# mLSTM branch output as four block pairs of seven half-size products, merged tiles kept on the chip

## The chip, the cores and the metric

The kernel runs on one core of a Trainium2 chip. The metric is the device time of one launch in microseconds.

## What is computed

A decoder layer for 1024 tokens and a width of 1024, one sequence. Cut to what bears on the change:

```python
mod = silu(c) @ w_ada + b_ada                      # shift, scale, gate
h = rms_norm(x, g_norm) * (1 + scale) + shift
xa, va, oa, za, ia, fa, qa, ka, vat, zb, ga, gb = split(h @ w_in)
xc = silu(causal_depthwise_conv(xa, w_conv, b_conv))
h_m = mlstm_chunkwise(q, k, v from xc and va; gates ia, fa)      # 4 heads of 256
h_m = rms_norm(sigmoid(oa) * h_m, g_mlstm_head) + skip_mlstm * xc
y_m = (h_m * silu(za)) @ w_out_mlstm               # 1024 x 1024 @ 1024 x 1024
o_a = softmax-weighted sum of three dilated window attentions   # 4 heads of 128
y_a = (o_a * silu(zb)) @ w_out_attn                # 1024 x 512 @ 512 x 1024
merged = sigmoid(ga) * y_m + sigmoid(gb) * y_a
out = rms_norm(x + gate * (merged @ w_out), g_final)
```

## The kernel before

Every large product is made in three passes (`three_pass`, L590): each factor is held as a high part, rounded to the matmul's type, and a low part, what is left, and TensorE adds high x high, high x low and low x high. ScalarE writes high parts (a copy), GpSimd (POOL) or VectorE (DVE) low parts (a subtraction of two tiles in SBUF).

The program is a sequence of stages, each with hand-written instruction lists for SyncE (loads), GpSimd, TensorE, ScalarE and VectorE; semaphores tie them. Setup makes h; the blocks stage makes 28 pairs of output tiles of 128 channels, each pair by seven products of half the size in the order 5, 1, 2, 4, 6, 7, 3 (12 matmuls each, with sums of the weights ahead of them and sums of the products behind: 84 matmuls where the plain way takes 96); the mixing stage runs the four mLSTM heads and the attention; then follow **merge** (L1890) and **finish** (L2131). The change touches the end of mixing and these two.

End of mixing. `turn_stats` (L1177) on SyncE's queue stores a head's two tiles of the mLSTM branch to DRAM (L1182) and loads the softmax statistics `ct` (L1184). From them VectorE and ScalarE (`weigh_groups`, `group_exp`, L1545) make the weights of the three attention groups, which go through DRAM and come back as `qm` and `vt` (L1193); VectorE scales and adds with them (L1787 to L1807).

Merge. TensorE first makes the gates' plain products for output tiles 0 and 1 (`first_pairs`, 192 matmuls), then for each of the eight tiles m the mLSTM product `um` (2 token halves x 8 contraction tiles x 3 passes = 48 matmuls of 128x512) and the attention product `ua` (24). SyncE loads the eight tiles `um_lo_raw` (L1936) once all of the mixing is done, then four `ua` tiles, weights (L1919) and gates (L1925). ScalarE makes the high parts of the tiles (`split_high`, L2039), weights (`branch_high`, L2033) and output weights (`out_high`, L2043); VectorE the low parts (L2085, L2089); GpSimd the weights' (L1965). VectorE's `merge_tile` (L2104 to L2108) multiplies both products by their gates and adds them in `num`; ScalarE's queue stores the merged tile to DRAM (L2074).

Finish. GpSimd's queue loads merged columns of 128 tokens back (L2187, L2203) and GpSimd splits them (L2178 high, L2181 low). TensorE multiplies by the output weights, 8 token tiles of 2 x 24 matmuls. Behind the first 24 stands the gate sum (L2214), which waits for three rows that SyncE loads (gate, bg, gf, L2160 to L2162) at

```python
        sp.wait_ge(proj, BRANCH_DONE)
```

where BRANCH_DONE is the last mLSTM product of tile 7; the last attention product comes after it. ScalarE's queue loads rows of x (L2241) two counts later.

Of the kernel before, what the change touches and what calls it, by code (L numbers as in the profile page):

```python
# [9 lines left out]
P = 128  # L10
# [22 lines left out]
PAIRS0 = MERGE0 + 2 * PLAIN + 2 * KT  # L33
# [10 lines left out]
TOTAL = PRODUCTS * PAIRS  # L44
BY_POOL = 2
# [1027 lines left out]
def mix(nc, a, sem, ps, T):  # L1073
# [71 lines left out]
    def sync(sp):  # L1145
# [32 lines left out]
        def turn_stats(i):  # L1178

            for q in range(2):  # L1180
# [260 lines left out]
    def scalar(act):  # L1441
# [183 lines left out]
        group_exp(HEADS - 1)  # L1625

    def vector(dve):
# [760 lines left out]
```

## Time and profile before

| | us |
|---|---|
| median of 3 runs | 1370.97 (1370.72 to 1371.75) |
| the profiled execution | 1371.11 |
| its span, first to last instruction | 1369.3 |
| TensorE busy in the span | 1345.7 (98%) |
| VectorE busy | 855.3 (62%) |
| ScalarE busy | 580.1 (42%) |
| GpSimd busy | 463.0 (34%) |
| mean granted TensorE clock | 0.999 |

The span lies 1.8 us under the execution's time. A busy time counts records, and records of matmuls overlap, so that a full TensorE may be short of its peak. The stages stand in the trace at these times: mixing ends with transposes at 1097.8, the merge stage runs from there to 1273.4, the finish from there to the end.

### The profile page before, as it was taken

How to read it: one execution, taken by the hardware profiler on the slowest of the kernel's cores; microseconds unless marked ns; L12 is line 12 of the kernel's file. 1: busy time of each engine (PE TensorE's matmuls, PEld its weight loads, DVE VectorE, ACT ScalarE, POOL GpSimd, SP SyncE). 2: the span in 40 equal slices, each digit the busy share in tenths (PEclk: the TensorE clock that was granted, in tenths of full speed). 3: DMA queues.
4: the chain of work that ended last, by engine and by line, in shares of the span. 5: the costliest groups of instructions: out<-in, count | busy, mean ns of one | idle time of the engine just before them, and what ended most of it. 6: DMA issues, size and time to landing. Idle time of an engine off the chain costs nothing.

```text
span 1369.3 us, 17469 instructions
## 1 busy us (share of the span) xinstructions
PE 1345.7 (98%) x6453; PEld 1126.9 (82%) x6453; DVE 855.3 (62%) x1472; ACT 580.1 (42%) x1016; POOL 463.0 (34%) x298
## 2 busy tenths in 40 slices
PE   8999999999999999999999999999999999999998
PEld 6888888888888888888898788889878887888886
DVE  7988766573745444535368757866875766434586
ACT  7663353343444344332545446354545534111122
POOL 0096555554545555543002200210120022222551
PEclk9999999999999999999999999999999999999999
DMA  8522323323234343337231841553172165453543
GB/s 316 196 82 95 132 99 123 123 93 115 101 123 139 123 143 134 139 112 228 73 83 48 231 93 32 161 148 94 48 227 67 33 241 205 128 187 140 173 138 108
DMA packets 65454, 180.52 MB, mean 132 GB/s; under 512 B 22001, under 2 KB 22129, under 8 KB 63318
## 3 DMA queue, kind: packets, MB, share of 16 engines
q1 hardware_dynamic: 61082, 166.64, 36.9%
q10 hardware_dynamic: 3168, 8.70, 1.9%
q0 software_dynamic: 1120, 4.06, 1.0%
q8 instruction: 52, 0.85, 0.3%
q14 instruction: 32, 0.26, 0.1%
HBM read 132.49 MB, written 46.89 MB: 131 GB/s over the span
## 4 chain that ended last, share of the span: by engine, by line
PE 87%; DVE 6%; ACT 3%; DMA 2%; issue 1%; SPq 0%; POOL 0%; ACTq 0%; DVEq 0%
PE banks L592 23%; PE banks L594 23%; PE banks L593 23%; PE banks L1265 4%; PE banks L1390 2%; PE banks L1400 2%; PE banks L1350 2%; PE banks L1356 2%; DMA wraw<-in_w_all 1%; PE banks L1339 1%; PE banks L1348 1%; PE banks L1409 1%; PE banks L584 1%; PE banks L556 1%; PE banks L1378 1%
## 5 line engine op out<-in xcount | busy, mean ns | idle before, releaser
L1248 POOL TENSOR_TENSOR wlo<-wraw,whi 128x1024 fp32r<-128x1024 f32 x28 | 72.1, 2575 | 436.5 <-ACT whi L1468 411.1
L718 POOL TENSOR_TENSOR wlo<-w_sum,whi 128x512 fp32r<-128x512 f32 x112 | 165.2, 1477 | 137.4 <-ACT whi L843 137.4
L592 PE MATMUL banks<-t_hi,whi 128*128 128x512 f32 x448 | 174.3, 389 | 0.0
L593 PE MATMUL banks<-t_lo,whi 128*128 128x512 f32 x448 | 174.3, 389 | 0.0
L594 PE MATMUL banks<-t_hi,wlo 128*128 128x512 f32 x448 | 174.3, 389 | 0.0
L989 DVE TENSOR_TENSOR c_sum<-c_sum,banks 128x512 f32<-128x512 f32 x196 | 134.4, 686 | 44.7 <-PE banks L594 30.6
L592 PE MATMUL banks<-h_hi,whi 128*128 128x512 f32 x416 | 162.0, 389 | 0.0
L594 PE MATMUL banks<-h_hi,wlo 128*128 128x512 f32 x416 | 161.9, 389 | 0.0
L593 PE MATMUL banks<-h_lo,whi 128*128 128x512 f32 x416 | 161.8, 389 | 0.0
L843 ACT ACTIVATE whi<-w_sum 128x512 fp32r<-128x512 f32 x112 | 70.5, 630 | 165.5 <-PE banks L594 100.7
L592 PE MATMUL banks<-whi,h_hi 128*128 128x512 f32 x256 | 100.2, 391 | 1.4 <-POOL wlo L1248 1.4
L594 PE MATMUL banks<-whi,h_lo 128*128 128x512 f32 x256 | 99.7, 389 | 0.0
L593 PE MATMUL banks<-wlo,h_hi 128*128 128x512 f32 x256 | 99.6, 389 | 0.0
L593 PEld LDWEIGHTS banks<-t_lo,whi 128*128 128x128 f32 x448 | 84.1, 188 | 17.5
L594 PEld LDWEIGHTS banks<-t_hi,wlo 128*128 128x128 f32 x448 | 84.1, 188 | 17.4
L592 PEld LDWEIGHTS banks<-t_hi,whi 128*128 128x128 f32 x448 | 84.1, 188 | 17.4
L592 PEld LDWEIGHTS banks<-h_hi,whi 128*128 128x128 f32 x416 | 78.1, 188 | 16.3 <-POOL wlo L1248 0.2
L594 PEld LDWEIGHTS banks<-h_hi,wlo 128*128 128x128 f32 x416 | 78.1, 188 | 16.3
L593 PEld LDWEIGHTS banks<-h_lo,whi 128*128 128x128 f32 x416 | 78.1, 188 | 16.2
L865 ACT ACTIVATE fin<-c_sum 128x1024 f32<-128x1024 f32 x56 | 79.4, 1467 | 2.4 <-DMA chunk_decay_rows<-wlast 2.3
L718 POOL TENSOR_TENSOR wlo<-wraw,whi 128x512 fp32r<-128x512 f32 x42 | 63.0, 1507 | 48.8 <-ACT whi L843 48.8
L718 POOL TENSOR_TENSOR wlo<-raw,whi 128x512 fp32r<-128x512 f32 x42 | 58.5, 1402 | 51.3 <-ACT whi L843 51.3
(374 smaller groups left out, 2904.8 us busy)
## 6 DMA issues: line engine op xcount, KB each, us to landing
wraw<-in_w_all SPq DMA_DIRECT2D x72, 512.0 KB, 4.3
raw<-in_w_all SPq DMA_DIRECT2D x28, 512.0 KB, 4.4
queries_keys<-fin SPq DMA_DIRECT2D x12, 1024.0 KB, 4.0
qa<-queries_keys SPq DMA_DIRECT2D x12, 768.0 KB, 13.7
s_wada<-in_w_ada_cols SPq DMA_DIRECT2D x16, 512.0 KB, 8.2
attn_values<-fin SPq DMA_DIRECT2D x6, 1024.0 KB, 4.0
tn<-attn_values SPq DMA_DIRECT2D x12, 512.0 KB, 10.1
sig_c<-merge_gates SPq DMA_DIRECT2D x6, 1024.0 KB, 6.4
```

The costliest lines, as they stand in the source:

```text
L592: t_.matmul(out, w_hi, x_hi, start=first, stop=False)
L593: t_.matmul(out, w_hi, x_lo, start=False, stop=False)
L594: return t_.matmul(out, w_lo, x_hi, start=False, stop=last)
L718: nc.gpsimd.tensor_tensor(wlo4[:, o % 4, :], source(r, j), whi4[:, o % 4, :].bitcast(F32), subtract).then_inc(s_split, 1)
L843: A(whi4[:, o % 4, :], source(r, j), ACT.Copy).then_inc(s_high, 1)
L865: A(fin[r % 2][:, j, :].rearrange("p (r u) -> p r u", r=d), c_sum[:, r % 2, j, :].rearrange("p (u r) -> p r u", r=d), ACT.Sigmoid if r < Q ...
L989: v.tensor_tensor(out, x, bank(r, j), ALU.add).then_inc(part_added, 1)
L1248: nc.gpsimd.tensor_tensor(to, wraw[:, q % 2, :], hi.bitcast(F32), ALU.subtract).then_inc(w_split, 1)
L1265: mm = t_.matmul(ps[:, h, :], w[:, to, k * P:(k + 1) * P], x[:, k, h * HALF:(h + 1) * HALF], start=(e == 0), stop=(e == 3 * KT - 1))
L1350: mm = t_.matmul(M2[:, 0:DH + 1], qm[:, d, c * P:(c + 1) * P], cst[:, d, :], start=(d == 0), stop=(d == 1))
L1356: mm = t_.matmul((M1, M2)[d][:, 0:DH + 1], kw[:, c % 2, d * P:(d + 1) * P], v1[:, c, 0:DH + 1], start=True, stop=True)
L1390: mm = t_.matmul(A0[:, u * 2 * P:u * 2 * P + b * P], qa[:, g % 2, 0, t * P:(t + 1) * P], qa[:, g % 2, 1, (t + 1 - b) * P:(t + 1) * P], sta ...
```

## The change

The mLSTM branch's output product is made like the blocks: four pairs of output tiles, seven half-size products each. Token-side factors are the quarters of the branch (4 contraction tiles x 512 tokens) and sums of them: VectorE makes four differences (L2231 of the changed kernel) and seven low parts (L2236), each of 128x2048, ScalarE seven high parts (L2137, L2142). For each pair VectorE makes four weight sums (L2239) and seven joins into the on-chip tile `umo` (L2254), then multiplies by the gate. The attention products follow for all eight tiles, and `merge_tile` adds them into `umo` in place. GpSimd splits token columns straight out of `umo`; the merged tensor in DRAM is gone. Mixing ends with tiles 0 to 5 of the branch loaded by ScalarE's queue (L1651) and 6 and 7 copied on the chip by SyncE's. The gates come in halves; the output weights' tiles are made in the order 4 to 7, 0 to 3. BRANCH_DONE is now the last attention product.

```diff
-PAIRS0 = MERGE0 + 2 * PLAIN + 2 * KT
+PAIRS0 = MERGE0 + 2 * PLAIN + KT
...
+BRANCH_PAIRS = range(PAIRS, PAIRS + KT // 2)
+OUT_ORDER = (4, 5, 6, 7, 0, 1, 2, 3)
...
         def turn_stats(i):
-            for q in range(2):
+            for q in range(2) if i < HEADS - 1 else ():
                 sp.wait_ge(um_done, i * 2 + q + 1)
                 sp.dma_start(um_d[i, q], xc[:, q, :]).then_inc(um_out[q], 16)
             sp.wait_ge(stat_out, (i + 1) * 16 * sum(STATS))
             sp.dma_start(ct[:].rearrange("p g c w -> p g (c w)"), stat_d.rearrange("g (p c) w -> p g (c w)", c=NCH)).then_inc(ct_in, 16)
+            for q in range(2) if i == HEADS - 1 else ():
+                sp.wait_ge(um_done, 2 * HEADS - 1 + q)
+                sp.dma_start(T["um_raw"][:, KT - 2 + q, :], xc[:, q, :]).then_inc(T["tile_in"][KT - 2 + q], 16)
...
-        group_exp(HEADS - 1)
+        act.wait_ge(out_turned, 4 * HEADS)
+        for q in range(2):
+            act.wait_ge(um_out[q], 16 * HEADS)
+        for k in range(KT - 2):
+            act.dma_start(T["um_raw"][:, k, :], um_d[k // 2, k % 2]).then_inc(T["tile_in"][k], 16)
...
+        def product(r, j):
+            o = at_product(r, j)
+            bank_free(o)
+            pe.wait_ge(s_split, o + 1)
+            if r == PAIRS:
+                pe.wait_ge(t_lo_done, low_count(j))
+            hi, lo = factors[j]
+            for k in range(KH):
+                cols = slice(k * P, (k + 1) * P)
+                mm = three_pass(t_, bank(r, j), whi4[:, o % 4, cols], wlo4[:, o % 4, cols], hi[:, k, :], lo[:, k, :],
+                                k == 0, k == KH - 1)
+            mm.then_inc(gprod, 1)
...
-        branch(um_at(0), 0, 0, KT, UM_BANKS)
-        branch(um_at(1), 1, 0, KT, UM_BANKS)
-        branch(ua_at(0), 0, KT, HEADS, UA_BANKS)
-        branch(ua_at(1), 1, KT, HEADS, UA_BANKS)
-        for m in range(2, KT):
-            branch(um_at(m), m, 0, KT, UM_BANKS)
-            branch(ua_at(m), m, KT, HEADS, UA_BANKS)
+        for r in BRANCH_PAIRS:
+            for j in ORDER:
+                product(r, j)
+        for m in range(KT):
+            attn_branch(m)
...
+        def gate(m):
+            dve.wait_ge(*((sig_done, 4 * PLAIN) if m < PLAIN else (sig_in[m % 2], 16 * (m // 2))))
+            dve.wait_ge(part_added, PRODUCTS * (PAIRS + m // 2 + 1))
+            v.tensor_tensor(umo[:, m, :], umo[:, m, :], sa[m], ALU.mult).then_inc(merged_half, 1)
...
+        T["shared"]["weigh_groups"](HEADS - 1)
+        branch_rows(range(KH))
+        dve.wait_ge(pv_kept, 12 * HEADS + 1)
+        difference(5, up_right, up_left[0])
+        low(1, up_left[0])
+        branch_rows(range(KH, KT))
+        difference(6, low_right[0], bt_raw[5], 5)
+        low(5, bt_raw[5])
+        for part in ("scale_two", "join_two", "join_third", "gate_attn"):
+            T["shared"][part](HEADS - 1)
+        dve.wait_ge(T["ua_done"], 2 * HEADS + 1)
+        weight_sums(PAIRS)
+        difference(4, low_left[0], bt_raw[6], 6)
+        low(2, low_left[0])
+        low(4, bt_raw[4])
+        low(6, bt_raw[6])
+        difference(7, low_right[0], up_right)
+        low(7, bt_raw[7])
+        low(3, low_right[0])
...
-    BRANCH_DONE = branch_done(um_at(KT - 1), 1)
+    BRANCH_DONE = branch_done(KT - 1, 1)
...
         sp.wait_ge(proj, BRANCH_DONE)
+        sp.wait_ge(merged_half, merged(KT - 1, 0))
         sp.dma_start(gate[:], acc_d).then_inc(row_in, 16)
...
-        pool.wait_ge(mg_out, 16 * KT)
-        pool.wait_ge(T["bw_split"], 2 * KT)
-        for b in range(2):
-            pool.dma_start(mr[:, b, 0:KT - 1], rows[:, 0:KT - 1, b * P:(b + 1) * P]).then_inc(m_in[b], 16)
-        pool.wait_ge(m_in[0], 16)
-        pool.wait_ge(merged_half, 4 * (KT - 1))
-        split(0, slice(0, KT - 1), mr[:, 0, 0:KT - 1], 1).then_inc(m_part, 1)
+        pool.wait_ge(merged_half, merged(KT - 1, 0))
+        split(0, slice(0, KT - 1), 1).then_inc(m_part, 1)
...
-        act.wait_ge(proj, BRANCH_DONE + 2)
+        act.wait_ge(proj, BRANCH_DONE)
```

ScalarE at the end of the heads. Before (`sg`, `tn`: sigmoids of the heads; L1545: the exponential of the softmax statistics; L2021: sigmoids of the merge gates; L2027: a weight's high part; L2039: tiles' high parts):

```order
L1489 ACTIVATE tn<-sg 128x1024 [waits v_turned,kept1,kept0]
L1545 ACT_TABLE_LOAD
L1545 ACTIVATE cw<-cw 128x24 [waits ct_arg]
L2021 ACT_TABLE_LOAD
L2021 ACTIVATE qa<-banks 128x512 [waits proj] x2
L2027 ACTIVATE whi<-wraw 128x1024 [waits w_in0,proj]
L2021 ACTIVATE qa<-banks 128x512 [waits proj]
L2027 ACTIVATE whi<-wraw 128x1024 [waits w_in1,proj]
L2021 ACTIVATE qa<-banks 128x512 [waits proj] x2
L2039 ACTIVATE um_hi_a<-um_lo_raw 128x1024 [waits tile_in0]
L2039 ACTIVATE um_hi_a<-um_lo_raw 128x1024 [waits tile_in1]
```

and in the changed kernel (L1567 the exponential, L2125 the sigmoids, L2131 the weight):

```order
L1511 ACTIVATE tn<-sg 128x1024 [waits v_turned,kept1,kept0]
L1651 DMA um_lo_raw<-mlstm_branch 128x1024 [waits um_out1,um_out0,out_turned]
L1651 DMA um_lo_raw<-mlstm_branch 128x1024 x5
L1567 ACT_TABLE_LOAD
L1567 ACTIVATE cw<-cw 128x24 [waits ct_arg]
L2125 ACT_TABLE_LOAD
L2125 ACTIVATE qa<-banks 128x512 [waits proj] x2
L2137 ACTIVATE up_left_hi<-um_lo_raw 128x2048 [waits tile_in2,tile_in3,tile_in1,tile_in0]
L2131 ACTIVATE whi<-wraw 128x1024 [waits w_in0,proj]
L2142 ACTIVATE bt_hi<-bt_lo_raw 128x2048 [waits t_raw]
L2125 ACTIVATE qa<-banks 128x512 [waits proj]
```

Six tile loads now stand ahead of the exponential, and high parts of 2048 columns between the sigmoids and the weights' high parts.

VectorE in the same place. Before (L1781: last of the small operations for the softmax weights; `num`, `ew`: attention of the last head):

```order
L1781 TENSOR_TENSOR cw<-cw 128x24 [waits dve_steps]
L1787 TENSOR_TENSOR num<-num,qm 128x1024 [waits cb_in]
L1787 TENSOR_TENSOR num<-num,qm 128x1024 [waits cb_in,dve_steps]
L1796 TENSOR_TENSOR num<-num 128x4x256 [waits dve_steps]
L1787 TENSOR_TENSOR ew<-ew,vt 128x1024 [waits cb_in,pv_kept,dve_steps]
L1801 TENSOR_TENSOR num<-num,ew 128x16x64 [waits dve_steps]
L1807 TENSOR_TENSOR szb<-szb,num 128x1024 [waits zb_done,ua_done]
L2085 TENSOR_TENSOR um_lo<-um_lo_raw,um_hi_a 128x1024 [waits b_hi_done] x6
L2085 TENSOR_TENSOR um_lo<-um_lo_raw,um_hi_b 128x1024 [waits b_hi_done] x2
```

and in the changed kernel (`bt`: differences of quarters; L2239: weight sums):

```order
L1809 TENSOR_TENSOR cw<-cw 128x24 [waits dve_steps]
L2231 TENSOR_TENSOR bt_lo_raw<-um_lo_raw 128x2048 [waits tile_in3,tile_in2,pv_kept,tile_in1,tile_in0]
L2236 TENSOR_TENSOR um_lo<-um_lo_raw,up_left_hi 128x4x512 [waits t_hi_done]
L2231 TENSOR_TENSOR bt_lo_raw<-um_lo_raw,bt_lo_raw 128x2048 [waits tile_in7,tile_in6,t_raw,tile_in5,tile_in4]
L2236 TENSOR_TENSOR bt_lo<-bt_lo_raw,bt_hi 128x2048 [waits t_hi_done]
L1815 TENSOR_TENSOR num<-num,qm 128x1024 [waits cb_in]
L1815 TENSOR_TENSOR num<-num,qm 128x1024 [waits cb_in,dve_steps]
L1824 TENSOR_TENSOR num<-num 128x4x256 [waits dve_steps]
L1815 TENSOR_TENSOR ew<-ew,vt 128x1024 [waits cb_in,pv_kept,dve_steps]
L1829 TENSOR_TENSOR num<-num,ew 128x16x64 [waits dve_steps]
L1835 TENSOR_TENSOR szb<-szb,num 128x1024 [waits zb_done,ua_done]
L2239 TENSOR_TENSOR num<-wraw 128x512 [waits s_split,pair_in0,ua_done]
```

and behind the other three weight sums:

```order
L2231 TENSOR_TENSOR bt_lo_raw<-um_lo_raw,bt_lo_raw 128x2048 [waits t_raw]
L2236 TENSOR_TENSOR um_lo<-um_lo_raw,low_left_hi 128x4x512 [waits t_hi_done]
L2236 TENSOR_TENSOR bt_lo<-bt_lo_raw,bt_hi 128x2048 [waits t_hi_done] x2
L2231 TENSOR_TENSOR bt_lo_raw<-um_lo_raw 128x2048
L2236 TENSOR_TENSOR bt_lo<-bt_lo_raw,bt_hi 128x2048 [waits t_hi_done]
L2236 TENSOR_TENSOR um_lo<-um_lo_raw,low_right_hi 128x4x512 [waits t_hi_done]
```

Four operations of 2048 columns stand ahead of the weighing (L1815 on), seven behind the weight sums.

SyncE's queue there, before:

```order
L1149 DMA wraw<-in_w_all 128x1024 [waits w_split]
L1182 DMA mlstm_branch<-xc 128x1024 [waits um_done] x2
L1184 DMA ct<-softmax_stats 128x3x16 [waits stat_out]
L1186 DMA group_weights<-cw 128x3x8 [waits cw_done]
L1193 DMA qm<-group_weights 128x1024 [waits coef_out]
L1193 DMA qm<-group_weights 128x1024
```

and in the changed kernel:

```order
L1168 DMA wraw<-in_w_all 128x1024 [waits w_split]
L1203 DMA ct<-softmax_stats 128x3x16 [waits stat_out]
L1206 DMA um_lo_raw<-xc 128x1024 [waits um_done] x2
L1208 DMA group_weights<-cw 128x3x8 [waits cw_done]
L1215 DMA qm<-group_weights 128x1024 [waits coef_out]
L1215 DMA qm<-group_weights 128x1024
```

The statistics' load is ahead of the two tiles, which go to `um_lo_raw` on the chip. At the start of finish, before:

```order
L1919 DMA wraw<-in_w_all 128x1024 [waits bw_split]
L1919 DMA wraw<-in_w_all 128x512 [waits bw_split]
L1922 DMA wo_c_raw<-in_w_out 128x1024 [waits merged_half]
L1925 DMA sig_c<-merge_gates 128x2048
L2160 DMA gate<-gate_products 128x1024 [waits proj,acc_out]
L2161 DMA bg<-in_b_gate 128x1024
```

and in the changed kernel:

```order
L1977 DMA wraw<-in_w_all 128x512 [waits bw_split]
L1990 DMA gate<-merge_gates 128x1024 [waits merged_half]
L1990 DMA y<-merge_gates 128x1024 [waits merged_half]
L2361 DMA gate<-gate_products 128x1024 [waits merged_half,proj,acc_out]
L2362 DMA bg<-in_b_gate 128x1024
L2363 DMA gf<-in_g_final 128x1024
```

The final rows wait for a merged tile as well, and `proj` there is the count behind the last attention product.

## Rows read from the trace of the kernel before

**Rows 1.** The page, part 1: busy us (share of the span) x instructions.

```profile
PE 1345.7 (98%) x6453; PEld 1126.9 (82%) x6453; DVE 855.3 (62%) x1472; ACT 580.1 (42%) x1016; POOL 463.0 (34%) x298
```

**Rows 2.** The timeline of ScalarE: start us, us, engine, line, operation, [idle before <-releaser].

```profile
1219.25 1.06 ACT L2033 ACTIVATE whi<-wraw 128x1024 fp32r<-128x1024 f32 x1 [10.25 <-PE banks L594]
...
1235.57 1.06 ACT L2033 ACTIVATE whi<-wraw 128x1024 fp32r<-128x1024 f32 x1 [10.25 <-PE banks L594]
```

**Rows 3.** Busy us (x instructions) by stretches; then granted clock, DMA share, GB/s.

```profile
200.00:250.00 50.00, 50.00 (x222) 41.42 (x221) 32.88 (x38) 18.71 (x28) 25.63 (x19) 1.00 0.29 106
...
1145.00:1170.00 25.00, 24.20 (x106) 19.40 (x105) 12.30 (x12) 7.32 (x9) 3.91 (x3) 1.00 0.54 197
1170.00:1220.00 50.00, 50.00 (x223) 41.39 (x222) 18.76 (x23) 8.79 (x10) 12.54 (x6) 1.00 0.48 163
```

**Rows 4.** The timeline of TensorE, 1095 to 1283.

```profile
1097.80 0.47 PE L592 MATMUL banks<-h_hi,whi 128*128 128x512 f32 x1
...
1141.50 0.39 PE L592 MATMUL banks<-um_hi_a,whi 128*128 128x512 f32 x1
...
1146.38 0.50 PE L592 MATMUL banks<-um_hi_b,whi 128*128 128x512 f32 x1 [0.64 <-DVE um_lo L2085]
...
1278.89 1.88 PE L2214 MATMUL banks<-gate,ones 128*128 128x512 f32 x4
```

**Rows 5.** The timeline of GpSimd (POOL): the first split for the output product.

```profile
1268.23 1.67 POOL L2178 TENSOR_TENSOR m_first<-wraw,zero 128x896 fp32r<-128x896 f32 x1 [2.54 <-DMA wraw<-merged]
1269.98 2.13 POOL L2181 TENSOR_TENSOR m_first<-wraw,m_first 128x896 fp32r<-128x896 f32 x1
```

**Rows 6.** The timeline of VectorE (DVE), 1200 to 1210.

```profile
1204.97 2.58 DVE L2089 TENSOR_TENSOR wo_c<-wo_c_raw,wo_c 128x1024 fp32r<-128x1024 f32 x1 [9.65 <-ACT wo_c L2043]
...
1208.90 0.69 DVE L2108 TENSOR_TENSOR num<-num,sig_c 128x512 f32<-128x512 f32 x1
```

**Rows 7.** The timeline of VectorE, 60 to 84.

```profile
66.66 2.35 DVE L925 TENSOR_TENSOR t_lo<-t_lo_raw,t_hi 128x1024 fp32r<-128x1024 f32 x2
...
74.64 10.16 DVE L925 TENSOR_TENSOR t_lo<-t_lo_raw,t_hi 128x1024 fp32r<-128x1024 f32 x5
```

**Rows 8.** The timeline of VectorE, 1098 to 1133: the last head's softmax weights.

```profile
1107.38 0.17 DVE L1773 TENSOR_TENSOR cw<-ct 128x8 f32<-128x8 f32 x1 [1.80 <-DMA ct<-softmax_stats]
...
1119.47 3.25 DVE L1787 TENSOR_TENSOR num<-num,qm 128x1024 f32<-128x1024 f32 x2 [10.17 <-DMA vt<-group_weights]
...
1131.00 1.23 DVE L1807 TENSOR_TENSOR szb<-szb,num 128x1024 f32<-128x1024 f32 x1
```

**Rows 9.** The timeline of ScalarE, 1098 to 1112.

```profile
1099.29 1.28 ACT L1545 ACT_TABLE_LOAD   x1
...
1109.54 1.09 ACT L2021 ACTIVATE qa<-banks 128x512 f32<-128x512 f32 x2
```

**Rows 10.** The timeline of GpSimd, 1200 to 1208.

```profile
1204.07 2.40 POOL L1965 TENSOR_TENSOR wlo<-wraw,whi 128x1024 fp32r<-128x1024 f32 x1 [9.64 <-ACT whi L2033]
```

**Rows 11.** GpSimd's line L718 over the span: duration ns min/median/max.

```profile
L718 POOL TENSOR_TENSOR wlo<-w_sum,whi x112: 1280/1292/3277, 75.8 to 604.1; 128x512 fp32r<-128x512 f32 x112
```

**Rows 12.** The timeline of SyncE's queue, 1265 to 1275: the final rows' issues.

```profile
1268.26 0.33 SPq L2160 DMA_DIRECT2D gate<-gate_products  x1
...
1269.11 0.43 SPq L2162 DMA_DIRECT2D gf<-in_g_final  x1
```

**Rows 13.** DMA issues, 1250 to 1290: KB each, median us to landing.

```profile
gate<-gate_products SPq DMA_DIRECT2D x1, 512.0 KB, 3.9
...
gf<-in_g_final SPq DMA_DIRECT2D x1, 512.0 KB, 5.6
```

**Rows 14.** DMA issues of 1098 to 1125, the same columns.

```profile
um_lo_raw<-mlstm_branch SPq DMA_DIRECT2D x8, 512.0 KB, 10.7
...
ct<-softmax_stats SPq DMA_DIRECT2D x1, 24.0 KB, 2.5
```

**Rows 15.** The timeline of SyncE's queue, 1098 to 1115.

```profile
1100.84 0.35 SPq L1149 DMA_DIRECT2D wraw<-in_w_all  x1
```

More of the change, by code:

```diff
@@ new lines, in merge @@
+    upper, lower = slice(0, KH), slice(KH, KT)
+    up_left, low_left, low_right = ((um_raw[:, ks, part], um_lo[:, ks, part])
+                                    for ks, part in ((upper, LEFT), (lower, LEFT), (lower, RIGHT)))
+    up_right = um_raw[:, upper, RIGHT]
+    (up_left_hi, low_left_hi, low_right_hi) = (T[n][:] for n in ("up_left_hi", "low_left_hi", "low_right_hi"))
+    bt_hi, bt_lo, bt_raw = ({j: T[f"bt{n}_{part}"][:] for n, j in ((1, 5), (2, 6), (3, 7), (4, 4))} for part in ("hi", "lo", "raw"))
@@ L1961, in gpsimd @@
[L1961 to L1965 removed]
+        load_attn_weights(4)
+        sp.wait_ge(merged_half, merged(1, 4))
+        for k in (2, 3):
+            load_out(k)
+        for m in range(4, KT):
+            if m + 1 < KT:
+                load_attn_weights(m + 1)
+            load_gate_b(m)
@@ L2081, in vector, with branch_rows, difference, low @@
         step = T["shared"]["step"]
-        def split_low(k):
+        def branch_rows(ks):
+            for k in ks:
+                dve.wait_ge(tile_in[k], 32)
+        def difference(j, x, y, first=None):
+            if first is not None:
+                dve.wait_ge(t_raw, raw_count(first))
+            v.tensor_tensor(bt_raw[j], x, y, ALU.subtract).then_inc(t_raw, 1)
+        def low(j, raw_):
+            hi, lo = factors[j]
+            dve.wait_ge(t_hi_done, high_count(j))
+            v.tensor_tensor(lo, raw_, f(hi), ALU.subtract).then_inc(t_lo_done, 1)
@@ new lines, in plus, with join @@
+        def plus(r, name, out, x, j):
+            dve.wait_ge(gprod, 1 + at_product(r, j))
+            dve.wait_ge(part_added, added_part(r, name) - 1)
+            v.tensor_tensor(out, x, bank(r, j), ALU.add).then_inc(part_added, 1)
+        def join(r):
+            c11, c12, c21, c22 = (umo[:, 2 * (r - PAIRS) + j, part] for j in range(2) for part in (LEFT, RIGHT))
+            dve.wait_ge(first_kept, r + 1)
+            plus(r, "u2", c21, c11, 6)
+            plus(r, "u4", c12, c21, 5)
+            plus(r, "c11", c11, c11, 2)
+            plus(r, "c22", c22, c12, 7)
+            plus(r, "v", c21, c21, 7)
+            plus(r, "c21", c21, c21, 4)
+            plus(r, "c12", c12, c12, 3)
@@ new lines, in vector @@
+        low(5, bt_raw[5])
[10 more added lines that the diff above has]
+        low(3, low_right[0])
+        for r in BRANCH_PAIRS:
+            if r + 1 in BRANCH_PAIRS:
+                weight_sums(r + 1)
+            else:
+                for k in range(HEADS):
+                    attn_low(k)
+            join(r)
+            for j in range(2):
+                gate(2 * (r - PAIRS) + j)
@@ L2208, in tensor @@
+        for t in range(1, NCH):
+            if t > 1:
+                pool.wait_ge(prod, 2 * t - 2)
+            split(t, slice(0, KT), t + 2).then_inc(m_split, 1)
     def tensor(pe):
@@ L2338 @@
     pairs += [[np.arange(c, c + P) for c in (DH * i, DH * i + P)] for i in range(1, HEADS)]
+    w_um = x["w_out_mlstm"][0]
+    for p in range(KT // 2):
+        for c in range(2):
+            w_all[PAIRS0 + 2 * (PAIRS + p) + c] = tiles(w_um[:, (2 * p + c) * P:(2 * p + c + 1) * P])
     for r, two in enumerate(pairs):
```

432 lines of the change are left out of this document (256 added, 176 removed).

## The prediction

> **What bounds it now.** The page comes first. TensorE is busy for 98% of the span [rows 1], so the time is the number of matmuls times their spacing, plus the places where TensorE stands idle. The record of one matmul says 389 ns, but the records overlap, so the spacing is read elsewhere: in the merge stage two ScalarE rows that each follow the end of an output tile stand at 1219.25 and 1235.57 [rows 2], 16.32 us for 72 matmuls, which is **0.2267 us** each. The table by stretches shows where TensorE has gaps [rows 3]: none from 1170 to 1220, with a granted clock of 1.00, but 0.8 us is missing in 1145 to 1170. TensorE's own rows name most of it [rows 4], a wait for VectorE's low part of the last mLSTM tiles, and they bound all idle time of the stage. From the first pairs (1097.80) to the gate sum (1278.89) stand 192 + 576 + 24 = 792 matmuls, 179.6 us by the spacing, against 181.1 us by the clock: **1.5 us**.
>
> **The product.** 8 tiles x 2 halves x 24 = 384 matmuls go, 4 pairs x 7 products x 12 = 336 come; all are 128x512. The attention product (192), the first pairs and the output product keep their counts. 48 x 0.2267 = **-10.9 us**, all of it on the path, since TensorE is full there [rows 3]. That the seven-product form can run without gaps is shown by the stretch 200 to 250, where the blocks keep TensorE at 50.00 of 50.00 with the same form. The old idle goes with the rows that made it: **-1.5 us**.
>
> **Traffic.** Eight stores of a merged tile and their reloads vanish. The first reload is in at 1268.2 and its split ends at 1272.1 [rows 5], while TensorE takes the first output matmul 24 matmuls, 5.44 us, ahead of the gate sum's 1278.89 [rows 4], at 1273.45. They are hidden; their going gains nothing. The price of their cover comes below, since the split now starts later.
>
> **Later pairs and the attention tiles.** For a pair VectorE has 4 sums and 7 joins of 512 columns at 0.69 us and two gates of 1024 at 1.18 [rows 6, 7]: 7.6 + 2.4 = 10.0 us, against 84 x 0.2267 = 19.0 us of TensorE. ScalarE and POOL have seven splits of 512 columns each, below 1.1 and 1.3 us apiece. An attention tile takes 5.44 us of TensorE and 2.8 us of VectorE, with at most two output-weight splits (2 x 1.18) beside: 5.2 us. I cost all this at nothing; the cover is thin only in the last case, where each microsecond more would show.
>
> **The first pair.** Its seven token-side factors must be made before TensorE needs them. Before, VectorE made eight low parts of 1024 columns; now 11 operations of 2048 columns, 2.35 us each by the pair of 1024-column operations at 66.66 [rows 7], 26 us in all. Four of them stand ahead of the last head's softmax weighing (from 1119.47 to 1132.2, 12.8 us [rows 8]), where VectorE now idles 10.17 us, and seven behind it. I follow the chain from the arrival of the softmax statistics, which I put at 1107, as before. VectorE's small operations end at 1109.3 and the first difference at 1111.6. ScalarE has its exponential, a table load of 1.28, two copies (1.09) [rows 9] and a high part of 2048 columns, twice 1.04, up to 1112.7. Then follow low part 1, difference 6 and low part 5 on VectorE (to some 1119), the weighing (to 1131.7) and four weight sums (to 1134.5). TensorE leaves the first pairs at 1141.50 [rows 4] and would take a new product every 12 x 0.2267 = 2.72 us, the seventh at 1157.8.
>
> Seven times 2.35 would end at 1151 if VectorE ran alone. But each product also needs the low part of one weight from POOL, and the two engines take turns: POOL's split at 1204.07 takes 2.40 and VectorE's, begun at 1204.97, takes 2.58, so that it ends 1.1 us after POOL's [rows 6, 10] (the same operation form takes 1.23 at 1131.00, [rows 8]). From 74.64 on, VectorE's operations of 1024 columns, five in a row, take 2.03 each beside POOL's splits of 512; such a split takes 1.29 at the median, and up to 3.28 [rows 7, 11]. Seven of each in turn are 7 x (2.35 + 1.29) = 25.5 us, up to 1160.0 against 1157.8: 2.2 us. The same turn at the first product, whose weight sum must pass ScalarE and POOL, I put at 1.1 more. **+3.3 us.** The lower bound is 0, when VectorE's 1151 holds. The upper is 9, when the statistics land 6 us later, since the chain is serial. I take the value in between because both ends of it, arrival and turns, are the nearest rows.
>
> A rule bears on this. The Trainium skill, SBUF — State Buffer, section SBUF: two separate sides, says that VectorE and GpSimd arbitrate for a port pair that is locked for a whole instruction, that a VectorE operation with two SBUF inputs against a GpSimd one that reads SBUF is such a case, and that the loser fully blocks. By that rule, the trace agrees (2.58 against 1.23), the 2048-column operations speak against this change: each holds POOL up for 2.35 us. If the two overlapped instead, the term would be 0 and the sum 3.3 us lower.
>
> **The end of the stage.** Two waits appear. First, POOL can split the first token tile only when tile 6 is merged, 5.44 - 2 x 0.69 = 4.1 us before TensorE ends tile 7's product; the split takes 3.9 us (1268.23 to 1272.11 [rows 5]), with VectorE's merging of tile 7 in its way. It ends between in time and 1.5 us late; I take 1.0. Second, the three final rows (gate, bg, gf). Before, they went out at 1268.26, when the last mLSTM tile was done and 5.2 us ahead of the output product [rows 12]; the gate sum reads them at 1278.89. Now that point is the last attention product, so they go out as TensorE begins the output product, together with two x_rows from ScalarE's queue. The three were all in after 6.45 us, the first after 3.9 [rows 12, 13]: some 1.27 us for each 512 KB. Five: 3.9 + 4 x 1.27 = 9.0 us, where the gate sum is wanted after 24 matmuls, 5.44 us. **+3.6 us**, which takes in the 1.0, as that delays the gate sum too. Lower bound 6.45 - 5.44 = 1.0, if x_rows come last; upper 5, if both waits add.
>
> **Sum.** The profiled execution took 1371.1 us (1369.3 of span and 1.8 around it), 0.1 above the median of the runs. 1371.1 - 10.9 - 1.5 + 3.3 + 3.6 = **1365.6 us**. A measurement of this kernel can tell about 0.2% from no change, 2.7 us: faster is below 1368.2, slower above 1373.7.
>
> **Rivals.** *The covers hold.* The factors are made in time and the rows pass x_rows: 1371.1 - 12.4 + 1.0 = 1359.7. For it speaks the idle of 10.17 us that four operations fill; against it the turns in [rows 6, 7, 10].
>
> *The waits eat it.* Statistics 3 us later and both waits at the end added: 1365.6 + 3.0 + 1.4 = 1370.0, no change.
>
> *The statistics come late, and it is slower.* Their load (24 KB, 2.5 us to landing alone [rows 14]) moves ahead of SP's two tiles and goes out at about 1101.5, behind the weight tile of 1100.84 [rows 15]. Beside it now run six tiles of 512 KB on ScalarE's queue from 1099.3, where its table load stood [rows 9]. Eight such tiles together took a median of 10.7 us to landing [rows 14]. VectorE's whole list, and ScalarE's exponential with the high parts behind it, queue for the statistics. My case is 1107; each later microsecond costs one. From a landing at 1115, 1365.6 + 8 = 1373.6, it is **slower**; at 1118, 1376.6. Against it: the six tiles are 3.1 MB, 7.9 us at 400 GB/s, in by about 1109 even if all go first.
>
> On this the Trainium skill, DMA: Bandwidth & Descriptors, section Queues, rings and completion order, has each DMA engine turn between queues after a packet of some 9 to 17 descriptors; by that the small load gets its share at each turn and lands before the tiles do. No row here shows two such queues side by side.
>
> *The change doesn't save its matmuls.* Excluded by the order of the program: 6405 instead of 6453.
>
> **Chances.** Covers hold 0.20; forecast (1362 to 1368.2) 0.42; waits eat it, within 0.2%, 0.22; late statistics 0.16. The range takes in the first two, all but the end of the third, and leaves the fourth out: 1359.7 to 1373.0. Faster by over 0.2%: 0.62, within 0.22, slower 0.16.
>
> **What would show it.** 48 records of matmuls fewer; the statistics' landing near 1107, then VectorE without idle until about 1160; 3 us of TensorE idle between 1141 and 1166, ended by POOL's splits of weights; none after that until the output product; there about 1 us for the token split and 2.6 at the gate sum, ended by the landing of gf or bg. Full stretches at both places would make the forecast too high; idle in pairs two to four, or statistics after 1110, too low.

## The result, and the profile after

Measured: 1373.58 us (median, 1370.65 to 1375.27) against 1371.75 us for the kernel before on the same chips (1370.12 to 1373.72): ratio 1.0014, interval 1.0007 to 1.0020. The change takes 48 matmuls out and makes the kernel **1.8 us slower**. The forecast was 1365.6 us in a range up to 1373.0. The result lies 0.6 above that range and just inside what I called no change; the interval of the ratio excludes a gain.

The busy time by stretches of the changed kernel, columns as in [rows 3]:

```profile
1145.00:1170.00 25.00, 20.63 (x86) 15.17 (x85) 20.81 (x15) 10.42 (x15) 20.24 (x9) 1.00 0.27 94
1170.00:1220.00 50.00, 50.00 (x221) 41.26 (x220) 30.19 (x34) 15.87 (x24) 26.21 (x19) 1.00 0.35 122
1220.00:1270.00 50.00, 50.00 (x218) 40.67 (x218) 45.18 (x51) 12.51 (x16) 14.12 (x13) 1.00 0.52 177
1270.00:1285.00 15.00, 11.27 (x33) 7.42 (x32) 3.44 (x5) 0.72 (x2) 4.25 (x2) 0.77 0.41 164
1285.00:1335.00 50.00, 50.00 (x223) 41.39 (x222) 38.00 (x55) 11.51 (x27) 22.04 (x10) 1.00 0.28 85
```

The seven-product form runs full where it runs in steady state (1170 to 1270). Two stretches don't: 4.4 us are missing between 1145 and 1170, where it was 0.8 [rows 3], and 3.7 us between 1270 and 1285, with a mean granted clock of 0.77. TensorE's timeline names the places, the first as the split for the first pairs, the next two in the first block pair, then the gate sum:

```profile
1119.27 0.50 PE L612 MATMUL banks<-h_hi,whi 128*128 128x512 f32 x1 [0.48 <-POOL wlo L1270]
```

```profile
1148.88 0.47 PE L612 MATMUL banks<-low_left_hi,whi 128*128 128x512 f32 x1 [2.02 <-issue]
```

```profile
1159.72 0.47 PE L612 MATMUL banks<-bt_hi,whi 128*128 128x512 f32 x1 [1.27 <-POOL wlo L2038]
```

```profile
1273.18 0.39 PE L614 MATMUL banks<-wo_c,m_first 128*128 128x512 f32 x1
1277.30 3.78 PE L2401 MATMUL banks<-gate,ones 128*128 128x512 f32 x4 [3.73 <-DMA gf<-in_g_final]
1280.09 1.42 PE L612 MATMUL banks<-wo_a,m_first 128*128 128x512 f32 x1
1281.31 0.63 PE L613 MATMUL banks<-wo_a,m_first 128*128 128x512 f32 x1
1281.73 0.63 PE L614 MATMUL banks<-wo_a,m_first 128*128 128x512 f32 x1
...
1283.01 0.63 PE L614 MATMUL banks<-wo_a,m_first 128*128 128x512 f32 x1
1283.44 0.43 PE L612 MATMUL banks<-wo_b,m_first 128*128 128x512 f32 x1
1283.71 0.40 PE L613 MATMUL banks<-wo_b,m_first 128*128 128x512 f32 x1
```

In the last fence the matmuls at 1281.31 and 1281.73 start 0.42 us apart instead of 0.2267: TensorE runs at the lower of its two clocks, 1.2 instead of 2.4 GHz, until 1283.4. Before, the gate sum (1278.89, [rows 4]) came with no idle and a full clock.

Landmarks give the account. In the profiled execution the heads happened to end 1.1 us earlier than before (their last transposes start at 1094.75; this point lies between 1094.7 and 1098.2 in all profiled executions below), so I count from them:

| stretch | matmuls | at 0.2267 us | took | over |
|---|---|---|---|---|
| first pairs and block pair 1, 1096.74 to 1166.20 | 276 | 62.6 | 69.5 | 6.9 |
| pairs 2 to 4 and attention, to 1267.84 | 444 | 100.6 | 101.6 | 1.0 |
| output product up to the gate sum, to 1277.30 | 24 | 5.4 | 9.5 | 4.0 |
| gate sum to the end, against 90.4 before | | | 93.7 | 3.3 |

Of the 6.9 us, 0.9 are lost in the first pairs and 6.0 in the block pair. 1371.1 - 10.9 - 1.5 + 6.9 + 1.0 + 4.0 + 3.3 - 1.1 = 1372.8 us, which is the profiled execution.

### The profile page after: what moved, and what is told of

It is laid out like the page before. It is cut to its first block and busy times, and to the rows that moved or that the text cites. A ratio compares the mean times of both kernels' runs of the same rounds, so it can differ in the third digit from the quotient of the medians.

```text
span 1371.0 us, 17506 instructions
## 1 busy us (share of the span) xinstructions
PE 1339.9 (98%) x6405; PEld 1119.0 (82%) x6405; DVE 905.7 (66%) x1511; ACT 595.3 (43%) x1039; POOL 481.5 (35%) x308
```

## Experiments

Since the end of the heads wanders by up to 3.4 us between executions, each run below is also read by two lengths of its profiled execution: **stage**, from the last head's transposes to the gate sum, and **tail**, from there to the end of the span. A ratio is to the kernel before on the same chips, for the changed kernel 1371.75. The other runs stand on three chips (e1 to e4; e5 to e8 and e11; e9 and e10), where the kernel before has medians between 1370.5 and 1371.5, so a difference of medians between these groups is good to about 1 us.

| | median us | ratio to before, 95% | stage | tail |
|---|---|---|---|---|
| before | | | 183.07 | 90.4 |
| changed | 1373.58 | 1.0014 (1.0007 to 1.0020) | 182.55 | 93.7 |
| e1 rows early | 1366.32 | 0.9970 (0.9958 to 0.9981) | 178.91 | 90.6 |
| e2 tiles wait | 1373.13 | 1.0016 (1.0007 to 1.0025) | 182.50 | 93.7 |
| e3 fill | 1370.31 | 1.0001 (0.9992 to 1.0010) | 182.91 | 90.7 |
| e4 before, rows late | 1374.37 | 1.0027 (1.0016 to 1.0038) | 185.28 | 92.0 |
| e5 ScalarE order | 1369.80 | 0.9992 (0.9983 to 1.0001) | 181.02 | 90.6 |
| e6 statistics early | 1362.75 | 0.9942 (0.9929 to 0.9954) | 175.32 | 90.4 |
| e7 e5 and e6 | 1366.77 | 0.9964 (0.9951 to 0.9976) | 176.74 | 90.6 |
| e8 no GpSimd | 1360.81 | 0.9925 (0.9911 to 0.9939) | 172.92 | 90.5 |
| e9 weights first | 1363.01 | 0.9939 (0.9927 to 0.9952) | 173.87 | 90.6 |
| e10 difference 7 early | 1362.03 | 0.9935 (0.9922 to 0.9949) | 174.38 | 90.6 |
| e11 fill in the pair | 1367.80 | 0.9974 (0.9964 to 0.9984) | 178.83 | 90.6 |

### The end: late rows, and the clock behind them

**e1**, the three rows early:

```diff
+        sp.dma_start(bg_[:], a["b_gate"].broadcast_to([P, D])).then_inc(T["row_in"], 16)
+        sp.dma_start(gf_[:], a["g_final"].broadcast_to([P, D])).then_inc(T["row_in"], 16)
         for m in range(4, KT):
...
-        sp.wait_ge(proj, BRANCH_DONE)
         sp.wait_ge(merged_half, merged(KT - 1, 0))
         sp.dma_start(gate[:], acc_d).then_inc(row_in, 16)
-        sp.dma_start(bg[:], a["b_gate"].broadcast_to([P, D])).then_inc(row_in, 16)
-        sp.dma_start(gf[:], a["g_final"].broadcast_to([P, D])).then_inc(row_in, 16)
```

> The changed kernel with bg and gf loaded from the second attention tile on and gate as soon as tile 6 is merged, instead of all three at the last attention product. Theory (rows late, and the idle TensorE then lost its clock): the wait of 3.9 us at the gate sum goes and the granted clock stays at 1.00 from 1270 to 1285, which gives back another 3.3 us: 1373.6 - 7.2 = 1366.4 us. Rival (the clock fell for another reason, such as the load of all engines in the stage): only the wait goes, 1369.7 us, and the clock still falls. Rival (another transfer takes the rows' place): no change.

Measured 1366.32 us, 7.3 below the changed kernel, and 6.8 below e2, which ran on the same chip and has the changed kernel's stage and tail. The gate sum waits for nothing and the clock holds there:

```profile
1270.00:1275.00 5.00, 5.00 (x23) 3.95 (x22) 0.87 (x1) 0.00 (x0) 4.44 (x4) 1.00 0.51 203
1275.00:1280.00 5.00, 5.00 (x21) 3.61 (x20) 3.42 (x5) 0.72 (x2) 0.30 (x1) 1.00 0.00 0
1280.00:1285.00 5.00, 5.00 (x23) 4.14 (x23) 3.05 (x4) 0.65 (x2) 3.04 (x2) 1.00 0.00 0
```

**e3**, TensorE kept busy while it waits (17 matmuls whose result nobody reads ahead of the wait for the rows):

```diff
         def gate_sum():
+            for _ in range(FILL):
+                nc.tensor.matmul(ps[:, 5, :], m_hi[0][:, 0, :], wo[0][0][:, 0:HALF], start=True, stop=True)
             pe.wait_ge(row_in, 48)
```

> The changed kernel with 17 more matmuls of 128x512, 3.9 us by their spacing, whose result nobody reads, ahead of the gate sum's wait. Theory (the clock falls because TensorE stands idle): the gate sum starts as late as before, but the granted clock stays at 1.00 and 3.3 us come back: 1370.3 us. Rival (the clock falls whatever TensorE does there): 1373.6 us or more, with the clock at 0.65 to 0.77 from 1275 to 1285.

Measured 1370.31 us. The stage is as long as in the changed kernel (182.91 and 182.55), so the rows come as late, but the tail is 90.7 instead of 93.7: 3.0 us were the clock's, and it was the idle TensorE that lost it there.

**e4**, the reverse, in the kernel before:

```diff
-        sp.wait_ge(proj, BRANCH_DONE)
+        sp.wait_ge(proj, BRANCH_DONE + 2)
         sp.dma_start(gate[:], acc_d).then_inc(row_in, 16)
```

> The kernel before with the three final rows issued at the last attention product, 5.4 us later, and nothing else. Theory: the gate sum waits 1.0 us (rows alone, 6.45 us from first issue to last landing, against 5.44) to 3.6 us (with both x_rows beside); above about 3 us of idle the clock falls too, for 3.3 us more: 1372.8 to 1378.6 us. Rival (rows are not what the gate sum waits for): within 0.5 us of before.

Measured 1374.37 us, 3.4 above before. One line of the old kernel reproduces both parts of the loss at the end and about half of its size: the stage is 2.2 us longer and the tail 1.7, against 4.0 and 3.3 in the changed kernel. The clock fell although the idle time is only 2.1 us; my "above about 3 us of idle" was wrong.

```profile
1283.07 2.51 PE L2214 MATMUL banks<-gate,ones 128*128 128x512 f32 x4 [2.08 <-DMA gf<-in_g_final]
...
1285.80 0.63 PE L593 MATMUL banks<-wo_a,m_first 128*128 128x512 f32 x1
1286.23 0.63 PE L594 MATMUL banks<-wo_a,m_first 128*128 128x512 f32 x1
```

### The first pair: what sets it

**e2**, ScalarE's six tile loads wait for the statistics (`act.wait_ge(ct_in, 16 * HEADS)` ahead of them).

> The changed kernel with ScalarE's six tile loads waiting until the softmax statistics have landed. Theory (statistics queued beside the tiles, 9.4 us to landing): they land about 2.5 us after their issue, VectorE's first low part starts some 3 us earlier (near 1111.5), and TensorE's stalls in the first pair fall from 6.5 to about 3.5 us: 1370.5 us. Rival (the turns of VectorE and GpSimd alone set the pace behind 1139): the stalls stay above 5.5 us and the time within 1 us of 1373.6. Rival (the tiles become late in their turn): the first difference waits for the tiles and the time doesn't change.

Measured 1373.13 us: no change, by the second rival. The statistics landed in 3.6 us instead of 9.4, so the tiles on ScalarE's queue were what delayed them. They landed 0.2 us behind the weight tile that SyncE's own queue has ahead of them. But the six issues (3.25 us) and the table load now stand between them and ScalarE's exponential, and the tiles land late; VectorE's first difference starts at 1114.32, where it was at 1111.53 in an execution that was 2.0 us earlier:

```profile
1106.41 0.16 DVE L1802 TENSOR_TENSOR cw<-ct 128x8 f32<-128x8 f32 x1
...
1110.63 0.18 DVE L1806 TENSOR_TENSOR cw<-cw,ct 128x24 f32<-128x24 f32 x1 [3.64 <-ACT cw L1567]
...
1114.32 2.29 DVE L2232 TENSOR_TENSOR bt_lo_raw<-um_lo_raw 128x2048 f32<-128x2048 f32 x1 [2.64 <-DMA um_lo_raw<-mlstm_branch]
```

**e6** takes the other way, on e1: SyncE's queue issues the load of the statistics ahead of the weight tile, and so ahead of the tiles.

```diff
+                if (i, p) == (HEADS - 1, 6):
+                    load_ct(i)
                 load(HEAD0 + i * CHUNKS + p + AHEAD)
```

(`load_ct` is the load of the statistics, taken out of `turn_stats`.)

> The early-rows version with the load of the last head's softmax statistics moved on SyncE's queue ahead of the weight tile, so that it goes out before ScalarE's six tile loads. Theory (late statistics hold up the whole chain): they land by about 1100, VectorE's first difference starts near 1107 instead of 1111.5, TensorE's stalls in the first pair fall from 7.4 us (waits and the half-speed stretch) to below 3: 1361 to 1363 us. Rival (ScalarE's order and the turns set the stalls): 1366 us, within 1.

Measured 1362.75 us, as the theory had it: the stage is 3.6 us shorter than e1's. The statistics are there 1.7 us after issue and VectorE starts its first difference 11.6 us after the transposes, against 16.8 in the changed kernel:

```profile
1109.74 2.29 DVE L2240 TENSOR_TENSOR bt_lo_raw<-um_lo_raw 128x2048 f32<-128x2048 f32 x1
```

The idle of 2.0 us ahead of the third product is gone.

**e5** and **e7** change ScalarE's order, on e1 and on e6. In the changed kernel the weight's high part for the third product (1145.58) stood behind the high part of difference 4, which waits for VectorE, and GpSimd's split behind it met VectorE each time:

```profile
1143.29 1.92 ACT L2142 ACTIVATE bt_hi<-bt_lo_raw 128x2048 fp32r<-128x2048 f32 x1 [2.39 <-DVE bt_lo_raw L2231]
1145.11 0.58 ACT L2125 ACTIVATE qa<-banks 128x512 f32<-128x512 f32 x1
1145.58 1.15 ACT L2154 ACTIVATE whi<-wraw 128x512 fp32r<-128x512 f32 x2
1146.63 0.62 ACT L2154 ACTIVATE whi<-num 128x512 fp32r<-128x512 f32 x1
1154.25 1.92 ACT L2142 ACTIVATE bt_hi<-bt_lo_raw 128x2048 fp32r<-128x2048 f32 x1 [7.01 <-DVE bt_lo_raw L2231]
...
1156.55 0.62 ACT L2154 ACTIVATE whi<-branch_sum 128x512 fp32r<-128x512 f32 x1
```

```profile
1146.28 5.79 POOL L2038 TENSOR_TENSOR wlo<-wraw,whi 128x512 fp32r<-128x512 f32 x2 [5.18 <-ACT whi L2154]
1152.04 3.33 POOL L2038 TENSOR_TENSOR wlo<-num,whi 128x512 fp32r<-128x512 f32 x1
1157.25 5.66 POOL L2038 TENSOR_TENSOR wlo<-branch_sum,whi 128x512 fp32r<-128x512 f32 x2 [1.88 <-ACT whi L2154]
```

```diff
         sum_high(6)
-        sum_high(4)
         first_sigmoid(1, 1, 0)
         weight_high(TOTAL + 2)
         weight_high(TOTAL + 3)
+        sum_high(4)
```

> The early-rows version with one more edit on ScalarE: the sigmoid of the last gate and the high parts of the weights of the third and fourth product stand ahead of the high part of difference 4, which waits for VectorE. Theory (the third product's 2 us of idle comes from ScalarE's order: its weight's high part stood at 1145.6 behind a high part that waits for a VectorE operation, and GpSimd's split then lost its turn): the weight's high part comes at about 1141.5, the idle of 2.0 us ahead of the third product goes, and the half-speed stretch after it too: 1366.3 - 2.1 - 2.4, between 1362 and 1364 us. Rival (VectorE's chain of 2048-column operations sets it alone): the idle moves to the fourth product, total within 1 us of 1366.3.

> Both: ScalarE's order and the early statistics, on the early-rows version. Theory: the gains add up as far as there is something left to gain: with all stalls of the first pair gone 1366.3 - 7.4 = 1359 us; I expect 1359 to 1361, and the granted clock at 1.00 throughout the stage. Rival (turns of VectorE and GpSimd bound the pair whatever comes first): above 1362.

Both missed: in the median e5 is 3.5 us above e1 and e7 4.0 above e6, in the stage 2.1 and 1.4 (e7's profiled execution, 1363.97, was the fastest of its five). The idle ahead of the third product does go, but a longer one appears ahead of the sixth:

```profile
1161.77 0.77 PE L612 MATMUL banks<-bt_hi,whi 128*128 128x512 f32 x1 [4.57 <-POOL wlo L2041]
1162.33 0.63 PE L613 MATMUL banks<-bt_lo,whi 128*128 128x512 f32 x1
1162.76 0.63 PE L614 MATMUL banks<-bt_hi,wlo 128*128 128x512 f32 x1
```

In e5 GpSimd's splits, made earlier, now push VectorE's two low parts (6.66 us for the pair, where it was 5.55) and difference 7 back. ScalarE waits for difference 7 with the sixth product's weight behind it, and GpSimd idles 7.38 us for that weight:

```profile
1146.04 0.62 ACT L2157 ACTIVATE whi<-num 128x512 fp32r<-128x512 f32 x1
1156.31 1.91 ACT L2145 ACTIVATE bt_hi<-bt_lo_raw 128x2048 fp32r<-128x2048 f32 x1 [9.66 <-DVE bt_lo_raw L2234]
...
1158.61 0.62 ACT L2157 ACTIVATE whi<-branch_sum 128x512 fp32r<-128x512 f32 x1
```

```profile
1148.60 3.33 POOL L2041 TENSOR_TENSOR wlo<-num,whi 128x512 fp32r<-128x512 f32 x1
1159.30 5.65 POOL L2041 TENSOR_TENSOR wlo<-branch_sum,whi 128x512 fp32r<-128x512 f32 x2 [7.38 <-ACT whi L2157]
```

The idle of 4.6 us brings the lower clock, too. In e7 TensorE idles 3.25 us at the same product, and the clock falls as well. So the wait was named right and its cure wrong: the sixth product is the one that counts, and the earlier ones only share out the same delay.

**e11** shows that from another side. Nine more matmuls, whose result is overwritten, fill the 2.0 us ahead of the third product in e1, after which e1's clock had dropped.

> The early-rows version with 9 more matmuls of 128x512 (2.0 us by their spacing), whose result is overwritten, in the 2.0 us in which TensorE waits for the third product's weights in the first pair. Theory (that idle too drops the clock, in some executions): the third product starts as late as before, but no half-speed stretch follows it, 2.0 to 2.6 us less where there was one: 1364 to 1365.5 us, ratio to the kernel before 0.9955, with the clock at 1.00 and matmuls 0.2267 us apart from 1149 to 1155. Rival (the half-speed stretch comes from something else, say the load of the other engines): matmuls 0.43 us apart from about 1150 to 1153 as before, 1366.3 us, ratio 0.997.

The clock held (1.00 in 1150 to 1155, 0.66 in e1), as the theory said, and nothing was gained: stage 178.83 against 178.91, and a median of 1367.80 us, above what either side had expected. The third to fifth product end earlier and the sixth starts where it did, 65.1 us after the transposes (65.2 in e1). The same stretch in e1, then in e11, and e11's sixth product:

```profile
1150.00:1155.00 5.00, 5.00 (x16) 3.94 (x17) 5.00 (x2) 0.00 (x0) 5.00 (x2) 0.66 0.01 3
```

```profile
1150.00:1155.00 5.00, 4.67 (x21) 3.56 (x20) 4.77 (x2) 0.19 (x1) 5.00 (x2) 1.00 0.02 9
```

```profile
1160.27 0.47 PE L612 MATMUL banks<-bt_hi,whi 128*128 128x512 f32 x1 [1.26 <-POOL wlo L2041]
```

**e8** takes GpSimd's splits of the first pair away but for 8 of 512 columns (that part of the weights' low parts is not computed).

> The early-rows version in which GpSimd makes only 8 of 512 columns of each weight's low part in the first pair (the rest of those low parts is left out of the computation), so that VectorE hardly meets it. Theory (the two take turns, each VectorE operation of 2048 columns then costing 3.4 instead of 2.3 us): VectorE's seven operations behind the weight sums end some 6 us earlier, about 1155 to 1157 instead of 1161.8, and TensorE's stalls fall by 2 to 4 us: 1362 to 1364 us. Rival (no mutual exclusion, the 1100-ns surplus has another cause): VectorE's operations keep their 3.3 us and the time 1366.

Measured 1360.81 us, all the stalls of the pair gone, more than I expected. VectorE's operations take 2.29 us each instead of 3.3:

```profile
1143.98 2.28 DVE L2240 TENSOR_TENSOR um_lo<-um_lo_raw,low_left_hi 128x2048 fp32r<-128x2048 f32 x1
1146.18 4.49 DVE L2240 TENSOR_TENSOR bt_lo<-bt_lo_raw,bt_hi 128x2048 fp32r<-128x2048 f32 x2
1150.60 2.28 DVE L2235 TENSOR_TENSOR bt_lo_raw<-um_lo_raw 128x2048 f32<-128x2048 f32 x1
...
1157.67 2.29 DVE L2240 TENSOR_TENSOR um_lo<-um_lo_raw,low_right_hi 128x2048 fp32r<-128x2048 f32 x1 [0.52 <-ACT low_right_hi L2141]
```

The surplus in the changed kernel (5.55 for two, 3.37 for one) was mutual exclusion with GpSimd. GpSimd's side shows it too: a split of only 8 columns that begins 0.1 us behind a VectorE operation lasts as long as that operation.

```profile
1150.69 2.25 POOL L2042 TENSOR_TENSOR wlo<-num,whi 128x8 fp32r<-128x8 f32 x1
```

Without the splits the stage is 6.0 us shorter (178.91 to 172.92). That takes in the splits' own time in the chain beside the turns; no run separates the two. By the Trainium skill, SBUF — State Buffer, section SBUF: two separate sides, the pair of ports is locked for a whole instruction and the loser blocks fully; the trace agrees (2.25 us for 8 columns, 3.37 instead of 2.28 for VectorE).

**e9** and **e10** go on from e6: the weights' high parts of the sixth and seventh product stand ahead of the high parts that wait for VectorE; e10 has difference 7 ahead of low part 6 besides.

```diff
-            if o == TOTAL:
-                sum_high(7)
-            if o == TOTAL + 1:
+            if o == TOTAL + 2:
+                sum_high(7)
                 branch_high(low_right_hi, low_right[0], range(KH, KT))
```

> The version with early rows and early statistics, with one edit in ScalarE's order: the high parts of the weights of the sixth and seventh product stand ahead of the high parts of difference 7 and of the last quarter, which wait for VectorE. Theory (where ScalarE makes a weight's high part behind a high part that waits for VectorE, TensorE pays): the 1.3 us of idle ahead of the sixth product, ended by GpSimd's split, goes and most of the 3.0 us of stalls in the first pair: 1360 to 1361.5 us. Rival (VectorE's last low parts, 7 and 3, then end the wait at the same time): the idle stays in length and is ended by VectorE, 1362.7 us.

> The same with difference 7 ahead of low part 6 on VectorE, so that ScalarE's high part of difference 7 is ready when VectorE comes to low part 7 (VectorE waited 2.0 us for it). Theory: the chain's last part gets 2 us shorter, all stalls of the first pair below 1 us in sum: 1359.5 to 1360.5 us. Rival (low part 6 then comes late, by 2.3 to 3.4 us): a stall ahead of the fifth product instead, no gain over the version without this edit.

Stages of 173.87 and 174.38, 1.5 and 0.9 below e6: the 1.3 us of idle at the sixth product are gone in both, smaller waits of 0.2 to 0.4 us stay. In the medians (1363.01 and 1362.03 against 1362.75) neither differs from e6 beyond the scatter of 5 executions, and both miss what I had expected of them; e10, with a stage 0.5 us longer than e9's, went by its rival. e6, e9 and e10 all beat the kernel before on their own chip by 7.5 us or more, and by the ratios the changed one by some 10.

## Why the prediction was wrong

Two steps failed, by nearly the same amount: the first pair was sized at half of what it cost, and the clock was put at nothing. 3.6 + 3.3, the 1.0 of the steady part, 0.4 at the rows and the heads' -1.1 are the 7.2 us between the forecast and the profiled execution.

- **The matmuls, -10.9 us: right.** With the rows early and GpSimd's splits away (e8), stage and kernel are 10.2 and 10.4 us shorter than before, where 12.4 were forecast with the old idle; the 2.3 us between are small waits, 0.9 of them in the first pairs and 1.0 in steady pairs and attention tiles, where I put nothing.
- **The final rows, +3.6: right.** 4.0 us up to the gate sum, with the split of the first token tile in time but for 0.2 us. gf landed 8.5 us after its issue (1268.81), so 9.3 after the first of the three issues, against my 9.0.
- **The clock, which I did not price: this step failed.** The text put 2.6 us of idle on TensorE at the gate sum and costed it as 2.6 us. The profile of before shows a clock of 1.00 in every stretch I read, and TensorE idles at most 0.8 us in them; it gave me no row for what a longer idle time costs beyond itself. It cost 3.0 (e3) to 3.3 us (tail). With this term alone the forecast would have been 1368.9.
- **The first pair, +3.3: the mechanism was right, the size half of what it was, and this step failed too.** 6.9 us by the account above. Of my two causes both hold: the splits and their turns (6.0 us of stage in e8) and the statistics' arrival (3.6 us in e6; they overlap). I put the arrival at 1107 "as before", 11.2 us after the transposes' 1095.8, and noted the tiles beside it only as a rival's; it came at 1109.6, 14.9 us after them. By my own price of 1 us for each, that is the 3.6 us that the term was short, but this agreement is in part luck. Counted from the transposes, VectorE's seven operations behind the weight sums begin at 45.1 us, 6.4 later than I had them: two of the four operations ahead of the weighing took 4.48 us beside GpSimd's splits of 1024 columns, where I took 2.35. The seven then took 21.9 us instead of my 25.5, since three of them ran at 2.3 us without a split beside them, and ended 2.8 us late.

```profile
1109.60 0.17 DVE L1801 TENSOR_TENSOR cw<-ct 128x8 f32<-128x8 f32 x1 [5.08 <-DMA ct<-softmax_stats]
...
1116.88 4.48 DVE L2231 TENSOR_TENSOR bt_lo_raw<-um_lo_raw,bt_lo_raw 128x2048 f32<-128x2048 f32 x1
1121.29 4.48 DVE L2236 TENSOR_TENSOR bt_lo<-bt_lo_raw,bt_hi 128x2048 fp32r<-128x2048 f32 x1
```

- **The rival "late statistics"** described what happened, though not far enough to make the kernel slower by itself.
- **Which sentence should have warned.** I computed that the tiles are in by 1109 "even if all go first" and took 1107; the last tile landed at 1109.4 and the 24 KB load at 1109.57, behind all of them: 9.4 us to landing against 6.1 at the median of the six tiles. The Trainium skill, DMA: Bandwidth & Descriptors, section Queues, rings and completion order, says that each engine turns between its queues after a packet; I read from it that the small load would get in early. The packets of this trace agree with the turns and not with my reading. SyncE's queue (q1) starts none until 1103.3, 3.5 us after the issue of the weight tile that it has ahead of the statistics (1099.76), while ScalarE's (q10) is busy from 1098.0; why so late stays open. Then the two share: the weight tile's 128 packets of 4 KB go out until 1106.7, among 187 of ScalarE's. The statistics are 384 packets of 64 B, from 1105.8 to 1109.1; from 1106 to 1108 they start no faster than ScalarE's packets of 4 KB (96 against 106), and only as these run out (the last at 1108.8) do they go quickly. So the small load waited behind a bulk load of its own queue, and then its small pieces shared with large ones about one for one. Ahead of both it took 1.7 us (e6), with the weight tile alone ahead 3.6 (e2). Queue, packets, MB and share of the 16 engines in 1098 to 1103, then in 1103 to 1106:

```profile
q10 hardware_dynamic: 482, 1.78, 95.3%
```

```profile
q10 hardware_dynamic: 197, 0.74, 66.2%
q1 hardware_dynamic: 130, 0.47, 38.6%
```

- **The rival "covers hold"** needed the first four operations to fit into VectorE's 10.17 us of idle; they stood behind the statistics in its order, started late and took 14.2 us (1111.53 to 1125.69).
- **What the change saved in traffic** was put at nothing, and the account above closes without such a term.

## What to carry to other kernels

An idle time that a change puts on a TensorE that was full can cost twice: its own length, and a stretch at half the clock behind it (1.7 us in e4, 3.0 to 3.3 in the changed kernel). Where it sits in front of work that waits for another engine anyway, the second part is free (e11); where TensorE is the bound afterwards, it is paid in full (e1, e3). Before costing a wait, look at what the waiting engine does next.

When a barrier count moves (here from the last mLSTM to the last attention product), every load that hangs on it moves too; take them off it one by one as their buffers come free. And a small load on which a whole in-order list depends goes out ahead of the bulk loads, those of its own queue and of the others, not beside them.

## What the runs showed that I had not expected

- The clock fell after idle times of 2.1 (e4), 3.25 (e7), 3.7 (changed), 3.8 (e2) and 4.6 us (e5), and at the third product after 1.9 to 2.0 in e1, e2 and e3, where the changed kernel with 2.0 us at the same place kept it. After 1.3 us or less it never fell in this stage. The half-speed stretch ends by itself, with matmuls back at 0.2267 us.
- Idle time is not all that goes with a fall. In five profiled executions (e2, e4, e6, e8, e10) the clock also fell in setup, at 28 to 29 us, until about 32. TensorE ran transposes of 128x128 and products of one column ahead of it, and in these five no idle time between 8 us and the fall is over 0.52 us; what brought it there stays open. The 250th matmul starts at 52.4 to 52.7 us in the others and at 53.8 to 54.0 in these five, so some 1.4 us of the wandering of the heads' end is this. In e6, TensorE's longest idle time there, and the stretch (columns as in [rows 3]):

```profile
26.50 1.95 PE L553 MATMUL banks<-cc,s_wada 128*128 128x1 f32 x16 [0.52 <-ACT s_xnT L414]
```

```profile
28.00:33.00 5.00, 5.00 (x22) 4.18 (x23) 4.83 (x11) 4.93 (x6) 0.00 (x0) 0.66 1.02 357
```

- The clock also carries much of the changed kernel's scatter: of its 15 executions the three with the lowest mean granted clock (0.994) took 1374.4 to 1375.3 us, and the two fastest (1370.7) had 0.998.
- Making the weights of the third and fourth product earlier made the kernel 3.5 to 4.0 us slower in the median (e5, e7); in the traces GpSimd's splits and VectorE's operations take turns, and the sixth product's came last.
- VectorE's 2048-column operations cost 2.29 us alone, 3.3 to 3.4 beside a 512-column split of GpSimd and 4.48 beside one of 1024 columns, and that split itself 2.9 to 3.3 instead of 1.29 [rows 11].
